# One decoder layer on one Trainium2 core: the end of the scan, the masks and the weight requests of the block behind it

## The reference, cut to what matters

```python
proj = xn @ w_in                       # z | xBC | dt | gmlp_u | gmlp_v
dt = softplus(dt_raw + dt_bias)        # 24 heads
y, h_new = ssd_scan(xs, dt, a, bm, cm, h0)   # chunked scan; h_new is an output
y = gated_rmsnorm(y + d_skip * xs, z, ssm_norm)
a_out = y @ w_a_proj
b_out = spatial_gating(u, v, gm_ws, gm_bs) @ w_b_proj
gates = sigmoid(xn @ w_gate + b_gate)
merged = gates[:, :1024] * a_out + gates[:, 1024:] * b_out
return merged @ w_out, ...
```

## Time and profile before

| | us |
|---|---|
| median of 3 runs (lowest, highest) | 2085.32 (2078.94, 2086.09) |
| profiled execution, its own time | 2082.61 |
| its span, first to last instruction | 2080.9 |
| TensorE busy | 1968.3 (95% of the span) |
| VectorE, ScalarE, GpSimd busy | 1033.5, 749.7, 394.9 |

### The profile page before, as it was taken

The page is one execution under the profiler, slowest core; times in us unless marked ns, Lnnn a source line. Parts: engine busy times, 40 slices in busy tenths (PEclk is TensorE's granted clock), DMA queues, the critical chain, the costliest instruction groups (busy, mean ns, idle before and its releaser), DMA issues. The chain is left out here.

```text
span 2080.9 us, 32851 instructions
## 1 busy us (share of the span) xinstructions
PE 1968.3 (95%) x12220; PEld 1747.1 (84%) x12221; DVE 1033.5 (50%) x1201; ACT 749.7 (36%) x1089; POOL 394.9 (19%) x510
## 2 busy tenths in 40 slices
PE   7999999999999999898999999999999899998995
PEld 5788899999888888788998789888788788877884
DVE  4215254552565656466113341335633675886775
ACT  4322122222334444443002121423412264774674
POOL 2000100000343444431111000000000122223225
PEclk9999999999999999989999999999999899999998
DMA  5122233333334334398546211344404568998987
GB/s 198 58 88 68 67 92 101 82 83 91 97 116 122 111 113 125 103 311 281 180 139 216 84 61 41 107 167 163 154 36 165 205 218 274 331 372 289 318 303 275
DMA packets 247476, 333.02 MB, mean 160 GB/s; under 512 B 16269, under 2 KB 163629, under 8 KB 247329
## 3 DMA queue, kind: packets, MB, share of 16 engines
q1 hardware_dynamic: 211268, 276.25, 39.5%
q0 software_dynamic: 7344, 25.38, 4.7%
q10 hardware_dynamic: 28768, 30.02, 4.1%
HBM read 255.30 MB, written 77.61 MB: 160 GB/s over the span
## 5 line engine op out<-in xcount | busy, mean ns | idle before, releaser
L3932 ACT ACTIVATE e_w_high<-big 128x2048 fp32r<-128x2048 f32 x94 | 176.4, 1911 | 46.4 <-PEq L3018 20.7
L279 PE MATMUL psum<-hT_high,t_w_high 128*128 128x352 f32 x576 | 186.9, 324 | 0.3 <-DVE t_w_low L1022 0.3
L281 PE MATMUL psum<-hT_high,t_w_low 128*128 128x352 f32 x576 | 185.6, 322 | 0.0
L280 PE MATMUL psum<-hT_low,t_w_high 128*128 128x352 f32 x576 | 185.6, 322 | 0.0
L4073 DVE TENSOR_TENSOR e_w_low<-big,e_w_high 128x2048 fp32r<-128x2048 f32 x64 | 144.0, 2288 | 33.1 <-ACT e_w_high L3932 26.2
L279 PE MATMUL psum<-hT_high,s_w_high 128*128 128x352 f32 x384 | 131.8, 343 | 0.0
L280 PE MATMUL psum<-hT_low,s_w_high 128*128 128x352 f32 x384 | 125.1, 326 | 0.0
L281 PE MATMUL psum<-hT_high,s_w_low 128*128 128x352 f32 x384 | 124.8, 325 | 0.0
L3811 PE MATMUL psum<-e_w_high,e_xT 128*128 128x512 f32 x272 | 107.4, 395 | 3.7 <-DVE e_xT L4069 3.0
L279 PEld LDWEIGHTS psum<-hT_high,t_w_high 128*128 128x128 f32 x576 | 108.1, 188 | 0.5 <-DVE t_w_low L1022 0.4
L280 PEld LDWEIGHTS psum<-hT_low,t_w_high 128*128 128x128 f32 x576 | 108.2, 188 | 0.0
(11 more groups left out here) (590 smaller groups left out, 4907.0 us busy)
## 6 DMA issues: line engine op xcount, KB each, us to landing
big<-in_w_expert_gate SPq DMA_DIRECT2D x32, 1024.0 KB, 8.3
big<-in_w_expert_up SPq DMA_DIRECT2D x32, 1024.0 KB, 11.0
big<-in_w_expert_down SPq DMA_DIRECT2D x32, 1024.0 KB, 13.3
t_w<-in_w_in SPq DMA_DIRECT2D x24, 512.0 KB, 4.6
m_gates<-gate_scr SPq DMA_DIRECT2D x22, 528.0 KB, 5.7
x_scr<-t_conv_out ACTq DMA_DIRECT2D x20, 512.0 KB, 4.3
gate_scr<-s_gate_tanh ACTq DMA_DIRECT2D x16, 528.0 KB, 3.4
scan_w<-in_w_gate SPq DMA_DIRECT2D x16, 512.0 KB, 4.1
```

The source lines that it names most:

```text
L279: nc.tensor.matmul(out, ah, w_h, start=start, stop=False)
L280: nc.tensor.matmul(out, ah, w_l, start=False, stop=False)
L281: return nc.tensor.matmul(out, al, w_h, start=False, stop=stop)
L3932: return nc.scalar.activation(dst, src, ACT.Copy)
```

## The change

In `stage_rows` the high and the low dt weights become one fixed operand of 64 columns (24 high, 8 zero, 24 low, 8 zero), so that two matmuls replace three; DVE adds the two halves of the result. At the scan's end the turns of the last steps go between parts of the last gate product, ACT's order is changed to suit, and the waits for the stores move into the next block. There, the last three masks go from DVE to GpSimd and `q_xdd_parts` is made before the differences; `m_w` gets a place in two state buffers, so its first load waits for two state stores; the last branch-B weights are asked for sooner.

```diff
 # stage_rows, TensorE
-                            mm = matmul3(nc, ps[0:H, 3 + n, 0:SLAB], wdth[:, k, :], wdtl[:, k, :],
-                                         hh[:, k, xs_], hl[:, k, xs_], k == 0, k == DK - 1)
+                            parts = wdts[:, k].rearrange("p a h -> p (a h)")
+                            nc.tensor.matmul(ps[0:2 * HS, 3 + n, 0:SLAB], parts, hh[:, k, xs_], start=(k == 0), stop=False)
+                            mm = nc.tensor.matmul(ps[0:2 * HS, 3 + n, 0:SLAB], parts, hl[:, k, xs_], start=False,
+                                                  stop=(k == DK - 1))
 # stage_rows, VectorE
+            nc.vector.memset(wdts[:].bitcast(F32)[:, :, :, H:HS], 0.0)
...
-            nc.vector.tensor_copy(dtT[:, 0:T].rearrange("p (n t) -> p n t", t=SLAB),
-                                  ps[0:H, 3:6, 0:SLAB]).then_inc(s_dte, 1)
+            dt_slabs = dtT[:, 0:T].rearrange("p (n t) -> p n t", t=SLAB)
+            nc.vector.tensor_copy(dt_slabs, ps[HS:HS + H, 3:6, 0:SLAB]).then_inc(s_dtl, 1)
+            dve.wait_ge(s_dtl, 1)
+            nc.vector.tensor_tensor(dt_slabs, dt_slabs, ps[0:H, 3:6, 0:SLAB], ALU.add).then_inc(s_dte, 1)
 # stage_ssd, SyncE
-            for gg in range(G):
+            for gg in range(2):
                 store_y(NC - 1, gg)
             sp.wait_ge(s_ho, 1)
             sp.dma_start(g.out["ssm_p"], ho).then_inc(g.s_out, g.stored())
-            for q in range(2):
-                sp.wait_ge(s_yst[q], 16 * (STEPS // 2))
-            sp.wait_ge(g.s_out, 16 * g.n_out)
+            for gg in range(2, G):
+                store_y(NC - 1, gg)
 # stage_ssd, TensorE (the last slab's product can be made in parts lo to hi)
-            for m in range(4):
-                after(4, m, turn)
-                if m < 2:
-                    gate(NC - 1, G + m)
-                if m == 1:
...
+            after(4, 0, turn)
+            gate(NC - 1, G)
+            after(4, 1, turn)
+            pe.wait_ge(s_h, STEPS + G)
+            pe.wait_ge(s_y1, STEPS)
+            pe.wait_ge(s_mn, STEPS)
+            for j in range(XF):
+                tr = nc.tensor.transpose(ps[:, YO + j // 4, (j % 4) * P:(j % 4 + 1) * P],
+                                         h[:, j // 3, (j % 3) * P:(j % 3 + 1) * P], g.ident[:])
+            tr.then_inc(s_ht, 1)
+            gate(NC - 1, G + 1, 0, 2)
+            after(4, 2, turn)
+            gate(NC - 1, G + 1, 2, 6)
+            after(4, 3, turn)
+            gate(NC - 1, G + 1, 6, DK)
 # stage_ssd, ScalarE
-            for m in range(4):
-                after(3, m, scale)
-                after(2, m, squares)
-                after(4, m, write)
-                if m < 2:
-                    read(NC - 1, G + m)
+            after(3, 0, scale)
+            after(2, 0, squares)
+            after(4, 0, write)
+            after(2, 1, squares)
+            after(3, 1, scale)
+            read(NC - 1, G)
+            after(4, 1, write)
+            after(3, 2, scale)
             act.wait_ge(s_ht, 1)
-            act.wait_ge(s_gm, 6 * NC)
+            act.wait_ge(s_gp, 1)
             nc.scalar.copy(ho.rearrange("p f n -> p (f n)"),
                            ps[:, YO:YO + 3, :].rearrange("p b t -> p (b t)")).then_inc(s_ho, 1)
-            for q in range(2):
-                act.wait_ge(s_gst[q], 16 * NC)
+            after(4, 2, write)
+            after(4, 3, write)
+            read(NC - 1, G + 1)
 # stage_sample_merge, places
+        wa = g.alias32("m_w", [P, XF, P], at - 2 * NB * N * 4)
...
-        wa = g.alias32("m_w", [P, XF, P], at)
 # stage_sample_merge, SyncE
-                    if q % 3 == 0 and f + 2 < DK:
+                    if q % 3 == 0 and f + 2 < DK - 1:
                         load_bw(f + 2)
...
+            for q in range(2):
+                sp.wait_ge(y_stored[q], 16 * (NC * G // 2))
             load_y(0)
...
-                if i >= XF - 2:
-                    load_y(i - XF + 3)
-            chunks_done(first_chunk[XF], first_chunk[XF] + 3)
-            sp.wait_ge(s_bst[2], 32)
+                if i == XF - 2:
+                    load_bw(DK - 1)
+                    load_y(1)
+            for i in range(XF):
+                if slot(i) >= RING - 2:
+                    sp.wait_ge(s_ho[slot(i)], 16 * (uses(i) + 1))
             for k in range(2):
                 load_a(0, k)
+            load_y(2)
+            chunks_done(first_chunk[XF], first_chunk[XF] + 3)
             chunks_done(first_chunk[XF] + 3, CHUNKS)
...
                 sp.wait_ge(s_bst[q], 48)
+                sp.wait_ge(gate_stored[q], 16 * NC)
 # stage_sample_merge, GpSimd (behind its masks of C, before the first decay)
+            pool.wait_ge(s_tb, 1)
+            pool.wait_ge(s_bs, 1)
+            for b in range(NB - 3, NB):
+                op = nc.gpsimd.tensor_tensor(bm[:, b, :], bs[:].bitcast(F32), mask4[:, b:b + 1].to_broadcast([P, G * N]), ALU.mult)
+            op.then_inc(s_bml, 1)
 # stage_sample_merge, TensorE, state(0)
-                    pe.wait_ge(s_bma, 1)
-                    pe.wait_ge(s_bmv, 1)
-                    pe.wait_ge(s_dif, 1)
+                    pe.wait_ge(s_bmf, 1)
+                    pe.wait_ge(s_bml, 1)
+                    pe.wait_ge(s_cb, 1)
 # stage_sample_merge, ScalarE
             b_high(0)
+            for q in range(2):
+                act.wait_ge(gate_stored[q], 16 * NC)
...
             act.wait_ge(s_bs, 1)
+            act.wait_ge(g.s_out, 16 * n_out)
             for b in range(NB - 3):
 # stage_sample_merge, VectorE: these two lines now stand ahead of the differences
+            dve.wait_ge(s_xh, 1)
+            stt(xs[:], xdd[:], a1, xh[:].bitcast(F32), ALU.mult, ALU.add).then_inc(s_xs, 1)
...
-            dve.wait_ge(s_xh, 1)
-            stt(xs[:], xdd[:], a1, xh[:].bitcast(F32), ALU.mult, ALU.add).then_inc(s_xs, 1)
-            dve.wait_ge(s_bs, 1)
-            for b in range(NB - 3, NB):
-                op = nc.vector.tensor_scalar(bm[:, b, :], bs[:].bitcast(F32), mask4[:, b:b + 1], None, ALU.mult)
-            op.then_inc(s_bmv, 1)
```

75 lines of the change are left out of this document (38 added, 37 removed).

## The result

The changed kernel takes 2073.81 us (median of 5 runs, 2071.51 to 2074.01) against 2084.18 for the kernel before (5 runs beside it). The ratio is 0.995, with a 95% interval of 0.9939 to 0.9962. So it is faster by 10.4 us, 7.9 to 12.7 by the interval, where the forecast said 15.5. The profiled execution took 2074.01 in its own time, with a span of 2072.3 (before: 2080.9).

A forecast was written before the change was run, and what follows sets the result against it. PE, busy 95% of the span, was taken as the bound, with the DMA engines also close to full before the merge. 3.8 + 6.0 + 5.7 = 15.5 us off 2085.32 gave 2069.8 us; 8-in-10 range 2061 to 2077.5.

The forecast's parts named there:

- the first rival, the DMA queue eats the stage: Block behind the scan: dt and hand-over gains stay, steps 3 to 5 give only 1.8 us; 2073.7 us, chance 0.22.
- steps 3 to 5: Set-up clock, masks and last column in the block behind the scan: together 5.7 us, limited by the DMA queue.
- The dt product: Step 1, stage_rows: 48 matmuls instead of 72, DVE's second pass covered; 3.8 us gained.
- The hand-over: Step 2, scan's end: no waiting for stores, turns inside the last gate product; next block starts 6.0 us earlier.
- The set-up at a higher clock: Step 3, next block's start: after only 1.8 us rest, small products run at full clock; 1.5 us gained.
- The masks: Step 4, block behind the scan: with three masks on GpSimd, uT_low starts 3.0 us earlier, ends 2.2 and 3.3.
- The last column: Step 5, before the merge: earlier last weights save 7.1 us waiting and 1.8 us half clock, unless the queue limits.
- a rival at 6 us and given 0.04: Slower: SP stands behind a state store, so the last gate comes 6 us later, removing step 5; chance 0.04.
- the 8 to 17 that I had named: Sign: prediction wrong if the merge begins under 8 or over 17 us earlier relative to the dt product's end; forecast 11.7.

The follow-up runs named there:

- A: The kernel before with only the dt product edit: 2078.25 us, ratio 0.9981.
- B: Changed kernel with the store waits back at the scan's end: 2072.76 us. In "B + 86.5", B is instead the next block's first small product.
- C: Changed kernel with the scan's last state store issued in the next block, behind the second branch-B weights: 2073.91 us.
- D: Changed kernel with the first branch-B weights split later, behind the decay factors on ACT and the clamped differences on DVE: 2072.35 us.
- E: Changed kernel with the three masks back on DVE: 2071.83 us. In "T to E", E is instead DVE applying the gate to the first merge product.
- F: Changed kernel with GpSimd's first state decay held until DVE has made all four uT_low: 2073.91 us.
- J: Changed kernel with SP's requests in the block behind the scan, and m_w's place, as before: 2072.89 us.
- G: Changed kernel with the third y load ahead of the state store's wait and the first merge weights: 2072.85 us.
- H: Changed kernel with the third y load and the last gate's load ahead of the state store's wait and first merge weights: 2066.83 us.
- I: Changed kernel with the last gate's request first, then the third y load, then the state store's wait and first merge weights: 2069.59 us.
- K: Changed kernel with the third y load and last gate ahead of wait and merge weights, and masks on DVE directly behind q_b_parts: 2067.30 us.

## Why the prediction was right, and where it was wrong

The time lies in the range of 2061 to 2077.5 given for 8 in 10, 0.8 us above the forecast's own (2066 to 2073), and the direction was right; the gain was smaller by a third, 10.4 us for 15.5. It is, to 0.1 us, the figure of the first rival, the DMA queue eats the stage (2073.7), and the rival's reason shows in the last column. The agreement is in part chance: the rival left 1.8 us to steps 3 to 5, the trace has them lose 2.2, and 2.6 us of the measured gain are in no piece that was cut.

1. **The dt product** was right: 3.76 us in the trace, 4.0 measured (A). DVE's copy and add (1.25 and 1.24 us) were covered.
2. **The hand-over** was right in size (6.27 for 6.0) and wrong in worth. "The waits that move are hidden in the next block" looked at instructions queued behind a wait, and not at the transfers that nobody waits for any more. They meet the next block's first loads: B, with the waits back, is 3.5 us longer here and only 1.5 us longer from T to E, with no difference in time that can be told.
3. **The set-up at a higher clock** was the wrong step in sign: +2.25 for -1.5. The sentence "so I expect the full clock" took the length of the rest for the cause. The clock was at 1.00 through the rest and fell during the small products. Of the 2.25 us, 1.1 are the two waits without a releaser (1.32 us against 0.21 before). Half clock covers 5.2 us ahead of the first turn, against 3.9 before; half of that difference, 0.7 us, is an estimate of its cost, and 0.64 of it stand in the 24 transposes alone. The last 0.4 stay open. C and B, which take the stores out of the block's start, bring the first turn back to 11.27 and 10.80; D, which takes the late weights out of ACT's way, does not.
4. **The masks** were wrong in sign too. The -1.53 us from the first to the third turn is not their gain: the first turn itself came 2.25 us later, and counted from the block's start the third came 0.7 us later than before (24.80 against 24.08). E, which only puts the masks back, has it at 23.07, so the move cost 1.7 us where it was to bring 3.0. The step assumed that DVE's operations beside GpSimd would be stretched by 0.7 us each, from the spread of rows 9. In fact the stretching comes as whole instructions' waits (E, F), and it fell mostly on `uT_low` beside the decays, a pair that I had not listed. A sign of it stood in the trace of before: its three masks took 0.47, 2.11 and 2.11 us, so 3.3 us of that row were waiting beside GpSimd's decays and not the masks' own work. Whoever moves the masks away leaves the decays to meet `uT_low`. What is won ahead of the last gate's request counts only where it brings that request forward, as it did in E and did not in F.
5. **The last column.** The weights' wait went, as forecast. The gate's did not: I had it land at 967.5 on the old time scale, 9.4 us after its old request; it landed at about 960.8, 10.1 us after a request at 950.75 which was, counted from the block's start, late: B + 86.5, against B + 81.2 before (958.08 less 876.91). The step that failed is the price of the merge weights ahead of that gate, "1.9 us more in front". The request comes 5.3 us later, since the wait for the state's store (5.0 us) stands with them, which the text had priced in a rival at 6 us and given 0.04; 4.1 us of it are the new order's, as J, with the old one, has its request at 946.38, B + 82.4. The transfer itself took 10.1 us, before 10.5, so little of the 3 us that the queue was to win back shows. G, H, I and J divide it: the old order and the new one come out alike (J), y alone is not it (G), the gate behind the wait and the weights is it (H), and the merge weights come next: in H their split starts 1.2 us behind the gate's use (957.99 and 956.75), and in I the merge waits for them. The half clock behind the gap, for which I had taken 0.9 us, was there in full and reached into the merge (1.1 us).

The merge begins 8.9 us earlier relative to the dt product's end (891.7 us behind it before, 882.8 after), inside the 8 to 17 that I had named, at its lower end. That is luck: from the dt turns to T the change touches nothing, and over 14 profiles this stretch takes 761.9 to 762.7 us in ten and 765.5 to 765.9 in four. The profile of before has the long one, that of after the short one; the long one is no mark of the kernel before, since D, I and K have it too. Without these 3.7 us the merge would begin 5.1 us earlier, outside what I had named, and that sign would have called the prediction wrong. Differences of a few microseconds between two profiles say nothing until they are cut at events around the edit.

The Trainium skill (GPSIMD Engine Reference, Key points), weighed in the prediction, warns of contention for DVE instructions with two SBUF inputs or in a 2-port mode; the sum by that rule would have lost 0.8. The traces agree with the warning and show more than was taken from it: `uT_low` is such an instruction, and it was the one that I had not counted. The Trainium skill (SBUF — State Buffer, SBUF: two separate sides) calls it an exclusive lock, where one instruction blocks the other whole instead of sharing. E and F agree: 0.47 or 2.11 us for the same mask, 1.25 or 2.95 for the same `uT_low`, 1.9 or 5.9 for the same decay. The values in between fit a wait for the rest of the other's instruction: with the change the second decay starts at 881.57 beside a `uT_low` that ends at 882.72, and takes 2.91 us, which is that wait of 1.15 and 1.9 of its own to within 0.15.

## What to carry to other kernels

A wait that you remove at a border may have kept the next block's DMA queue clear; price the stores that stay in flight, and not only the engines behind the wait. In a list that issues in order, ask of each request what stands in front of it, waits as well as bytes, and put first the one whose data the bottleneck needs first: here having the request of 528 KB, and the y load, ahead of 768 KB and a 5 us wait was worth as much as the dt edit (4.2 us on the mean of four kernels against eight). Before you move work to GpSimd, look at what DVE runs next to it and next to what GpSimd does afterwards: here products with two SBUF inputs stood still beside it, and so did the masks, which have one.

## What the runs showed of the hardware that was not expected

- The granted clock stayed at 1.00 through a rest of 1.5 us and fell to 0.50 in the stretch of small matmuls behind it, which PE filled (2.00 us busy in 2, 866 to 868). Behind the rests of 5.1 (B) and 6.9 us (before) the 128 transposes took 5.2 and 5.0 us, with no shorter time behind 1.5 (5.4 in C): each time part of them ran at 0.50.
- In the block's start PE stood still for 0.3 to 1.0 us with no releaser in the profile ("issue"), twice with the change (1.32 us) and in D (1.4), once in C (0.8), where one store is out of the way, once and for 0.21 us before, and not at all in B, where the queue is empty when the block begins. A full DMA queue alone is not enough for it: the share was 1.19 around the long wait (874 to 875), but also 1.21 around the short one before (885 to 886) and 1.20 in B (872 to 873), which has none. The profile's DMA view has one packet of 16 KB of the kind "instruction" that ends 1.4 to 1.5 us ahead of PE's restart each time (867.6 to 868.5 and 872.7 to 873.9 with the change; 883.3 to 884.5 before). That speaks for a wait for PE's own instructions, but B has such packets without a rest, for which engine they are is not shown, and nothing was tried on it.
- GpSimd and DVE block each other by whole instructions: a decay of 1.9 us lasts 5.9 beside an unbroken row of four DVE products with two SBUF inputs, and one such product of 1.25 us lasts 2.95 beside a decay.
